# Two activation halves in one 512-column matmul: the column form of a two-layer model block

## The reference, cut to what matters

```python
# first block
z = rms_norm(x) @ w_in                    # q, k, v, gate and four convolution inputs
x = x + concat(y_attn, y_conv) @ w_out
x = x + sigmoid(rms_norm(x) @ w_ple_gate + b) * rms_norm(p @ w_ple_proj)
# second block
proj = rmsnorm(x) @ w_in_2                # xr, q, ckv, qi, ki, wi, gr, ga
mixed = sigmoid(gr) * rg_lru(conv(xr)) + sigmoid(ga) * dsa_attention(...)
x = x + mixed @ w_o
# peer: 8 heads pick 16 of 16384 experts for each token
q = xn @ peer_wq;  s1 = q1 @ keys1.T;  s2 = q2 @ keys2.T;  top_k ...
z = xn . peer_u[e];  y = (gelu(z) * gate) @ peer_v
return rmsnorm(x + y)
```

## Time and profile before

| | |
|---|---|
| runs | 2859.31, 2858.69, 2858.67 us (median 2858.69) |
| profiled execution | span 2859.0 us; no other time of it is given |
| TensorE busy | 2794.1 us, 98% |
| VectorE busy | 1742.8 us, 61% |
| ScalarE busy | 1338.5 us, 47% |
| GpSimd busy | 233.8 us, 8% |
| granted TensorE clock, mean | 0.989 |
| column-form matmuls | 3 x 3984, 128 x 256 columns each |

### The profile page before, as it was taken

One profiled execution on the slowest core, in us unless ns is written; L12 is line 12 of the kernel. 1 busy time (PEld: TensorE's weight loads), 2 busy tenths in 40 slices (PEclk: granted clock), 3 DMA queues, 4 the chain that ended last, 5 costly groups with the idle time before them and its releaser, 6 DMA issues.

```text
span 2859.0 us, 54803 instructions
## 1 busy us (share of the span) xinstructions
PE 2794.1 (98%) x18524; PEld 2576.8 (90%) x18524; DVE 1742.8 (61%) x2688; ACT 1338.5 (47%) x1868; POOL 233.8 (8%) x340
## 2 busy tenths in 40 slices
PE   8999999899999999999999999999999999999998
PEld 6899977789999999889999999999997888888886
DVE  6665655656976555578886666555554555555555
ACT  5444445545664334455555444444444444444444
POOL 0000000000000000000004887000000000000000
PEclk9999999999999999999999999999999999999999
DMA  6544454554454444455564444655655555555555
GB/s 244 191 141 164 159 176 151 172 199 141 169 172 160 153 147 148 168 192 187 186 205 167 157 157 164 203 204 204 207 205 176 191 194 194 191 192 194 193 191 191
DMA packets 153406, 514.71 MB, mean 180 GB/s; under 512 B 17040, under 2 KB 33680, under 8 KB 152208
## 3 DMA queue, kind: packets, MB, share of 16 engines
q1 hardware_dynamic: 131904, 482.54, 49.7%
q10 hardware_dynamic: 21456, 31.60, 3.2%
HBM read 501.49 MB, written 12.58 MB: 180 GB/s over the span
## 4 chain that ended last, share of the span: by engine, by line
PE 96%; DVE 2%; ACT 1%; issue 1%; DMA 0%; POOL 0%; DVEq 0%; ACTq 0%; SPq 0%; POOLq 0%
PE bank L451 17%; PE bank L452 17%; PE bank L453 17%; PE bank L1924 8%; PE bank L1925 8%; PE bank L1926 8%; PE bank L471 5%; PE bank L472 4%; PE bank L473 4%; PE bank L1900 2%; PE bank L1804 1%; PE bank L1799 1%; PE bank L1783 0%; PE bank L1823 0%; PE bank L1836 0%
## 5 line engine op out<-in xcount | busy, mean ns | idle before, releaser
L428 DVE TENSOR_TENSOR w_lo<-raw,w_hi 128x1024 fp32r<-128x1024 f32 x904 | 1100.4, 1227 | 959.2 <-ACT w_hi L419 955.7
L419 ACT ACTIVATE w_hi<-raw 128x1024 fp32r<-128x1024 f32 x904 | 954.0, 1058 | 1232.1 <-PE bank L453 649.7
L451 PE MATMUL bank<-act_hi,w_hi 128*128 128x256 f32 x3984 | 1147.2, 288 | 5.7 <-DVE w_lo L428 1.9
L452 PE MATMUL bank<-act_lo,w_hi 128*128 128x256 f32 x3984 | 1130.0, 284 | 0.0
L453 PE MATMUL bank<-act_hi,w_lo 128*128 128x256 f32 x3984 | 1129.8, 284 | 0.0
L451 PEld LDWEIGHTS bank<-act_hi,w_hi 128*128 128x128 f32 x3984 | 767.1, 193 | 12.5 <-issue 9.5
L452 PEld LDWEIGHTS bank<-act_lo,w_hi 128*128 128x128 f32 x3984 | 767.4, 193 | 0.9
L453 PEld LDWEIGHTS bank<-act_hi,w_lo 128*128 128x128 f32 x3984 | 766.9, 192 | 0.0
L1924 PE MATMUL bank<-w_hi,act_hi 128*128 128x512 f32 x1024 | 399.0, 390 | 3.8 <-DVE act_lo L1581 3.8
L1925 PE MATMUL bank<-w_lo,act_hi 128*128 128x512 f32 x1024 | 399.1, 390 | 0.0
L1926 PE MATMUL bank<-w_hi,act_lo 128*128 128x512 f32 x1024 | 399.0, 390 | 0.0
(11 more groups left out here) (265 smaller groups left out, 1648.6 us busy)
## 6 DMA issues: line engine op xcount, KB each, us to landing
raw<-in_stream SPq DMA_DIRECT2D x904, 512.0 KB, 3.3
big<-in_ukv ACTq DMA_DIRECT2D x16, 512.0 KB, 4.0
z_kept<-cst ACTq DMA_DIRECT2D x64, 128.0 KB, 1.7
cst<-z_kept ACTq DMA_DIRECT2D x64, 128.0 KB, 2.9
big<-in_x SPq DMA_DIRECT2D x2, 1024.0 KB, 9.2
big<-in_rows ACTq DMA_DIRECT2D x2, 1024.0 KB, 6.0
big<-in_rg_w ACTq DMA_DIRECT2D x1, 2048.0 KB, 8.3
x_kept<-big ACTq DMA_DIRECT2D x1, 2048.0 KB, 6.6
```

Of the source, the lines that this page charges most:

```text
L419: act.activation(w_hi[:, s, :], raw[:, s, :], ACT.Copy).then_inc(hi_ready, 1)
L428: dve.tensor_tensor(w_lo[:, s, :], raw[:, s, :], w_hi[:, s, :].bitcast(F32), ALU.subtract).then_inc(lo_ready, 1)
L451: pe.matmul(out_ap, hi, act_hi[:, k, :], start=(k == 0), stop=False)
L452: pe.matmul(out_ap, hi, act_lo[:, k, :], start=False, stop=False)
```

## The change

`act_hi` and `act_lo` become the two halves of one buffer `act2`, side by side for each tile. A step of the column form becomes two matmuls: `hi` by both halves at once, 512 columns into the whole bank, and `lo` by the high half into the bank's first half. The bank then holds two partial sums. ScalarE copies the second half to SBUF (`low_half`), and VectorE adds the bank's first half to that copy (`add_halves`), in the order of blocks, which one counter (`summed`) follows. Where tanh or gelu was applied straight from the bank, ScalarE now waits for the sum and applies it in SBUF. The semaphores of the single uses go, and everyone who waited for them waits for `summed`. In `conv` two banks that VectorE read directly are copied and added like the others.

```diff
+        act2 = sb("act2", [P, KT, 2, S], F32R)
+        act_hi = act2[:, :, 0, :]
+        act_lo = act2[:, :, 1, :]
...
-                    pe.matmul(out_ap, hi, act_hi[:, k, :], start=(k == 0), stop=False)
-                    pe.matmul(out_ap, hi, act_lo[:, k, :], start=False, stop=False)
-                    mm = pe.matmul(out_ap, lo, act_hi[:, k, :], start=False, stop=(k == KT - 1))
+                    pe.matmul(bank[:, :], hi, act2[:, k, :, :].rearrange("p a n -> p (a n)"), start=(k == 0),
+                              stop=False)
+                    mm = pe.matmul(bank[:, 0:S], lo, act_hi[:, k, :], start=False, stop=(k == KT - 1))
                 mm.then_inc(unit_done, 1)
+
+        def low_half(act, dest, bank):
+
+            act.activation(dest, bank[:, S:2 * S], ACT.Copy).then_inc(low_ready, 1)
+
+        def add_halves(dve, dest, bank, block):
+
+            dve.wait_ge(low_ready, block + 1)
+            dve.tensor_tensor(dest, dest, bank[:, 0:S], ALU.add).then_inc(summed, 1)
+
+        def wait_summed(eng, block):
+
+            eng.wait_ge(summed, block + (SUMMED_AT_START + 1))
...
-            act.activation(KWT, banks[2][:, 0:S], ACT.Copy).then_inc(kwt_kept, 1)
+            low_half(act, KWT, banks[2])
...
-                act.activation(TG, banks[0][:, 0:S], ACT.Tanh, scale=0.5).then_inc(gr_tanh, 1)
+                low_half(act, TG, banks[0])
+                wait_summed(act, block_of("heads", h, 2, 0))
+                act.activation(TG, TG, ACT.Tanh, scale=0.5).then_inc(gr_tanh, 1)
...
-                act.activation(GZ[:, n, :], banks[2 + n][:, 0:S], ACT.Gelu).then_inc(gelu_ready[n], 1)
+                low_half(act, GZ[:, n, :], banks[2 + n])
+                wait_summed(act, block)
+                act.activation(GZ[:, n, :], GZ[:, n, :], ACT.Gelu).then_inc(gelu_ready[n], 1)
                 act.wait_ge(gelu_ready[n], b2 + 2)
...
-                    act.activation(PQS[:, a, :], banks[a][:, 0:S], ACT.Copy).then_inc(pq_kept[a], 1)
+                    low_half(act, PQS[:, a, :], banks[a])
...
-            for k in range(2):
-                ahead(split_lo, dve, "kiwi", 0, 2, k)
+            ahead(split_lo, dve, "kiwi", 0, 2, 0)
+            add_halves(dve, KWT, banks[2], block_of("kiwi", 0, 1, 0))
+            ahead(split_lo, dve, "kiwi", 0, 2, 1)
...
+            def keep_z(part, i, per, k):
+
+                add_halves(dve, GZ[:, k % 2, :], banks[2 + k % 2], block_of(part, i, per, k))
+
             for h in range(PH):
-                ahead(split_lo, dve, "wqu", h, 4, 0)
                 for a in range(2):
-                    ahead(split_lo, dve, "wqu", h, 4, 1 + a)
+                    ahead(split_lo, dve, "wqu", h, 4, a)
+                    add_halves(dve, PQS[:, a, :], banks[a], block_of("wqu", h, 4, a))
+                for a in range(2):
+                    if a:
+                        ahead(split_lo, dve, "wqu", h, 4, 2)
+                        keep_z("wqu", h, 4, 2)
                     dve.wait_ge(ps_kept[a], h + 2)
...
                 ahead(split_lo, dve, "wqu", h, 4, 3)
+                keep_z("wqu", h, 4, 3)
...
                         if s % 4 == 3:
                             ahead(split_lo, dve, "u_gates", i, 2, n, units=(s // 4,))
+                    keep_z("u_gates", i, 2, n)
...
                 for a in range(2):
-                    pe.wait_ge(pq_kept[a], h)
-                    columns_out(pe, pair_of("wqu", h, 4, a), a, banks[a][:, 0:S], fills=6)
+                    wait_summed(pe, block_of("wqu", h, 4, a - 4))
+                    columns_out(pe, pair_of("wqu", h, 4, a), a, banks[a], fills=6)
                 for a in range(2):
-                    pe.wait_ge(pq_kept[a], h + 1)
+                    wait_summed(pe, block_of("wqu", h, 4, a))
                     pe.wait_ge(ps_kept[a], h + 1)
```

More of the change, by code:

```diff
@@ L79 @@
 UNITS = 2 * PAIRS
+HALVED = {}
+_n = 0
+for _name, _count in [("conv", 4 * CONV_J), ("kiwi", 1), ("qi", IH * ID // P), ("rnn", 2 * KT), ("heads", 2 * H2),
+                      ("wqu", 4 * PH), ("u_decode", 2 * PH), ("u_gates", S // 8), ("u_late", NB // 2)]:
+    HALVED[_name] = _n
+    _n += _count
+SUMMED_AT_START = 4
 CONST = {}
@@ L437, in pair_of, with block_of, columns_out @@
             return i * per + (FIRST[part] + k)
-        def columns_out(pe, pair, odd, out_ap, units=(0, 1), fills=None):
+        def block_of(part, i, per, k):
+            return i * per + (HALVED[part] + k)
+        def columns_out(pe, pair, odd, bank, units=(0, 1), fills=None):
             for u in units:
@@ L1132, in _ @@
                         ahead(split_lo, dve, "conv", j, 4, 0)
+                        add_halves(dve, CS, banks[0], block_of("conv", j, 4, 0))
                         att_scores(j, g)
                         dve.wait_ge(conv_gate, j + 1)
-                        dve.scalar_tensor_tensor(out=CG, in0=CG, scalar=1.0, in1=banks[0][:, 0:S], op0=ALU.add,
+                        dve.scalar_tensor_tensor(out=CG, in0=CG, scalar=1.0, in1=CS, op0=ALU.add,
                                                  op1=ALU.mult).then_inc(conv_gate_used, 1)
@@ L1498, in _, with keep_decode @@
             lows = iter(range(2 * PH))
+            def keep_decode(k):
+                ahead(split_lo, dve, "u_decode", 0, 2, k)
+                keep_z("u_decode", 0, 2, k)
             def more(count=1):
                 for _ in range(count):
-                    ahead(split_lo, dve, "u_decode", 0, 2, next(lows))
+                    keep_decode(next(lows))
             cv = CV.rearrange("p h t k -> p (h t) k")
@@ L1550, in _ @@
                 ins.then_inc(picks_ready, 1)
-            for _ in lows:
-                ahead(split_lo, dve, "u_decode", 0, 2, _)
+            for k in lows:
+                keep_decode(k)
             dve.wait_ge(slots_kept, 3)
@@ L1571, in _ @@
                     ahead(split_lo, dve, "u_late", i, 2, n)
+                    keep_z("u_late", i, 2, n)
                     dve.wait_ge(gelu_ready[n], i + (EARLY // 2 + 1) + 1)
@@ L1859, in _, with experts_in @@
             turn_rows(3, 5)
-            def experts_in(pair, b2, n, units=(0, 1)):
+            def experts_in(pair, block, n, units=(0, 1), back=2):
                 if units[0] == 0:
-                    pe.wait_ge(gelu_ready[n], b2 + 1)
-                columns_out(pe, pair, n, banks[2 + n][:, 0:S], units)
+                    wait_summed(pe, block - back)
+                columns_out(pe, pair, n, banks[2 + n], units)
             pe.wait_ge(keys_ready, 16)
@@ L1878, in _ @@
                     ins.then_inc(ps_made[a], 1)
-                    experts_in(pair_of("wqu", h, 4, 2 + a), h, a)
+                    experts_in(pair_of("wqu", h, 4, 2 + a), block_of("wqu", h, 4, 2 + a), a, back=4)
             with pe.Fori(0, PH) as i:
                 for n in range(2):
-                    experts_in(pair_of("u_decode", i, 2, n), i + PH, n)
+                    experts_in(pair_of("u_decode", i, 2, n), block_of("u_decode", i, 2, n), n)
             for a in range(2):
```

120 lines of the change are left out of this document (68 added, 52 removed).

## The result

The changed kernel takes 2866.04 us (median of nine runs, 2860.24 to 2874.17), the kernel before, run beside it, 2859.31 (2858.04 to 2862.04). The ratio is 1.0022, with a 95% interval of 1.0014 to 1.0031: slower by two thousandths, where 2827 us (2811 to 2847) and a gain were forecast.

The account below looks back on a forecast made before the run. It took TensorE, paced by its instructions, as the bound. From 2859.0 us, -53.1 saved, +12.0 query stage, +0.9 entering u_decode, +1 u_decode, +3 u_gates and +4.1 single costs gave -32.1: 2827 us, range 2811 to 2847.

Parts of the forecast that it names:

- I take 13.3: All column-form steps: one matmul fewer saves its fixed 13.3 ns, 346.7 in place of 360.0 ns, 53.1 us in all.
- Rivals 3 and 4: Column-form steps: fixed part stays, 2870 us, chance 0.06; or only 1.5 to 3 ns goes, 2859 to 2865, chance 0.03.
- Query stage, +12.0: wqu: VectorE's adds and its wait behind ScalarE's gelu make a head 24.8 us against 23.08, seven intervals, +12.0 us.
- rival 2: Query stage: TensorE's 1.7 us stall drops its clock, +9 us more, 2836 and up to 2848 us; chance 0.15.
- u_gates, +3 (0 to +8): u_gates: late one-hot rows stall TensorE 0.1 to 0.2 us in every other pair or so, +3 us.
- u_decode, +1 (0 to +3), and its entry, +0.9: u_decode: 16 adds among long one-hot operations, VectorE within half a microsecond, +1 us; VectorE enters behind, +0.9 us.
- rnn, "nothing; +10.9 at most": rnn: VectorE's 32 adds grow its work to 175.2 us, in a stage of 194.2, so no cost; at most +10.9.
- heads, nothing (+0.4 at its end): heads: the chain grows by an add, covered by at least one further block of 5.55 us; +0.4 us at the end.
- Once each, +4.1: Single costs: after kiwi +1.9, ends of qi +0.4, conv +0.6, heads +0.4, u_late +0.8; together +4.1 us.
- rival 1: Whole kernel: VectorE keeps up and the adds hide, leaving only u_gates and the ends; 2810 to 2816 us, chance 0.17.
- Rival 5: conv, heads, rnn: handshakes eat each block's 0.213 us, 96 blocks, +20; 2847 us, up to 2856; chance 0.06.

Follow-up runs that it names:

- e1: Kernel before with the wide matmul but its old way out, without adds (high-by-low products computed, left out): 2819.49 us, ratio 0.9857.
- e4: Changed kernel with ScalarE's wait for the sum moved behind other work in wqu, u_gates and u_decode: 2847.15 us, ratio 0.9946 to the kernel before.
- e8: Changed kernel with VectorE in rnn adding block 0's halves before the next pair's second-unit w_lo: 2861.62 us, ratio 1.0009 to the kernel before.
- e3: Kernel before with the change only in conv, kiwi, qi, heads and u_late: 2842.96 us, ratio 0.9935.
- e9: e4 plus e8's order and u_decode's last gelu behind the copies of the picks, widths alternating: 2836.28 us, ratio 0.9923 to the kernel before.
- e10: e9 with matmul widths ordered 512, 512, 256, 256 in each two steps: 2834.64 us, ratio 0.9914 to the kernel before.
- e5: Changed kernel with each unit's eight 512-column matmuls first, then its eight 256-column ones: 2865.03 us, ratio 1.0017 to the kernel before.

## Why the prediction was wrong, step by step

- **"I take 13.3, since at full clock both widths show it."** Right at one of two paces (346.7), half right at the other (353.3). The term of -53.1 measured -44.5 in the profiled execution of the changed kernel and -41.6 alone in e1. The prediction had said that no row shows the two widths in turn, and the way they alternate is what failed. Rivals 3 and 4 fall. Over the 320 ns that 768 columns take at 2.4 GHz, a step's two matmuls cost 26.7 or 33.3 ns. The Trainium skill, "TensorE: Matmul & The Clock Gate", section "Wait — 56ns, not 53.3ns?", gives about 2.5 ns a matmul, an estimated 5 for the two; no run agrees with it.
- **Query stage, +12.0.** Measured 12.5: +7.1, and the stretch's 29 blocks had saved 5.4. Chain, stall and new wait were as told, and the clock stayed at 1.00, so rival 2 falls. e4 shows its largest part to be the order on ScalarE: with the score copy ahead of the gelu a head takes 23.4 to 23.6.
- **u_gates, +3 (0 to +8).** The step that failed worst, by size: 12.3 (+7.1, and 5.2 saved), and 2.8 more before the first one-hot matmul. The chain was told well: from the w_hi that the prediction calls H, rows done at H + 7.9, measured H + 8.0 (w_hi at 1610.36, rows to 1618.36). The due time was wrong: I asked when TensorE needs the last of the four rows, but it stood at the first, at H + 7.2, while the first row was done near H + 7.2 (1617.19 + 0.36) and took until 1617.83 to release it; and a loop's turn right behind the wait cost 0.34 more in the median. 0.71 a turn in place of 0.2.
- **u_decode, +1 (0 to +3), and its entry, +0.9.** Measured 6.2 (+3.6, and 2.6 saved). Adds were counted, but not that ScalarE's next w_hi waits behind the gelu for them: VectorE and ScalarE then take turns, and each long operation of VectorE's shows. e4 recovers 3.5.
- **rnn, "nothing; +10.9 at most".** Measured 3.0 (-0.7, and 3.7 saved). The cover was a mean over the stage, 175.2 of 194.2; in the rounds with top-k VectorE has 12.3 us of work where TensorE wants 11.96. e8 recovers 2.2 by order alone.
- **heads, nothing (+0.4 at its end).** Measured 2.4: the first head pays once, its interval 19.41 where 17.77 stood, and later heads nothing beyond the pace. The end, where +0.4 was forecast, cost 2.4: TensorE waits 3.9 us for the last head's probabilities in place of 1.5.
- **Once each, +4.1.** conv 1.2, u_late 1.35, and some 5 in all else: 1.7 after kiwi, where 1.9 was forecast, and the 2.4 at the end of heads, while the next wait, ahead of `w_o`, is 0.7 shorter (1.9 in place of 2.6). What is left isn't traced to a wait: the kernel up to its first column-form matmul and everything behind u_late, where no column-form matmul runs, are 1.2 us longer each, and vary by 1.7 and 1.2 among the thirteen traces. Undersized, on the right side.
- **Readings.** The overlap of 0.08 on VectorE isn't in the four w_lo in 4.87 us, which give 0.02; the price of 0.34 for an add held all the same (1612.82 to 1613.15 above). The adds of conv and heads are 64, not 48, and rival 1's bounds come to 2810 to 2814. None of this changes the sum.

Rival 5 named the mechanism in rnn and heads, but at the price of every block; it binds in a few. The mechanisms were mostly the ones written down; u_gates, u_decode, rnn and heads were each sized far too low, and with the second pace that is the error. What stays open: why the alternating widths have two paces and what picks one. The same u_late ran at 346.7 in the changed kernel, e1, e3, e8 and e9 and at 353.3 in e4, so the stage's own code doesn't decide it; once begun, the pace is kept. Of the units that begin right behind one-hot matmuls (193 in the traces of the changed kernel, e1, e3 and e4, nearly all in u_gates), a first 256-column matmul 312 to 314 ns behind the first of 512 led to 346.7 in 76 of 79, and 315 to 319 ns behind to 353.3 in 66 of 67. The other 47, with 320 ns and more, went either way (23 and 24), and in the other stages the first distance doesn't tell the paces apart. The spread of the runs fits two paces: 13.9 us in the changed kernel, 13.3 in e8, 10.3 in e4 and 8.5 in e9 (5.6 in e3, 3.5 in e1's four), against 4.0 in the kernel before and 2.0 to 6.0 in the five kernels with twos or eights. e4's six runs lie in two groups, 2838.6 to 2839.8 and 2847.0 to 2848.9, about the 6.8 of u_late apart. But only one run of each kernel has a trace.

## What to carry to other kernels

When two engines that work in order must both touch a result, look at what stands behind the wait, not at the length of the added operations: moving one waiting gelu behind other work gave back 22 us in three stages (e4, which lost 1 of it again ahead of u_gates), with all 249 adds of 0.41 us in place. Slack must be read in the round or turn that has the least of it, and at the first item that a consumer needs. And a saving worked out from two instructions, each measured among its own kind, is to be checked where the two alternate; here two or eight of a kind at a time (e10, e5) kept it steady.

## What the runs showed of the hardware

- In these traces alternating 512- and 256-column matmuls have two stable paces, 346.7 and 353.3 ns a step, kept for up to 1024 steps; 512, 512, 256, 256 shows one (348.4), and eight of each one (349.3).
- TensorE's loop turn costs nothing visible in u_gates while TensorE has no wait just before it (0.03 us to the next matmul in the kernel before, as in the middle of a turn), and 0.34 us right behind a wait (median of 16 turns, 0.29 to 0.39); in e4, where that wait is mostly gone, 0.03.
- A GpSimd one-hot row takes 782 ns beside VectorE's work before the change, and 809 (changed kernel) to 846 (e10) beside more of it; that the one causes the other is argued.
